# Normalising softmax probabilities on GpSimd before they are turned, in a fused decoder layer

## The chip, the core and the metric

One core of a Trainium2 chip. The time is that of one execution of the whole program in microseconds; lower is better. The kernel before takes 305.01 us, the median of three runs (304.72 to 305.29).

## The reference, cut to what matters

One decoder layer for 256 tokens of width 1024, 16 heads of 64. One projection gives q, k and v. Heads 0 to 7 (group g = 0) attend causally, heads 8 to 15 (g = 1) through a mixture of dilated windows. At this length both are a softmax over a masked row of at most 256 keys:

```
p = softmax(q k^T / 8 + mask)          per head and query
o = p v
o = rmsnorm(o over the group's 512 columns) * gain
x = x + concat(o of both groups) w_out
x = x + (silu(h w_gate) * (h w_up)) w_down,  h = rmsnorm(x) * gain
out = rmsnorm(x) * gain
```

## The kernel before, in words

**Weights.** All products with weights are done in three passes of TensorE: w_hi and w_lo are a rounded weight and its rest, x_hi and x_lo the same of the activation, and hi\*hi, hi\*lo and lo\*hi are added in PSUM (`three_pass`, L431 to L433). Weights come as blocks of 128x512. Blocks 0 to 47 are w_in (six groups of columns of eight blocks; the first four blocks alternate between the first two groups), 48 to 55 w_out for group 0, 56 to 63 for group 1, the rest the feed-forward part. A ring of twelve slots holds them. SP loads four at a time (a quad, `ring_quad`, L356), waiting for lo_ready; ScalarE rounds a pair of blocks (L719), VectorE subtracts (L935, lo_ready), TensorE multiplies (blk_done). ScalarE works nine blocks ahead of its step and VectorE seven.

**Attention.** q and k are rotated on VectorE (`rotate`, L985 to L993: two products into rope_a and rope_b, one sum into rot), turned by TensorE (L458) and split again (L804, L807, L1010, L1013). A tile is 128 queries by 512 columns of scores: tiles 0 and 1 of a group hold four heads each with 128 keys (the first half of the queries), tiles 2 to 5 two heads each with 256 keys. A score item u makes tiles 2u and 2u + 1 in PSUM banks 4 and 5 (L479, L482 to L484). VectorE adds the mask and takes the maximum (L1028, probs, max_ready), ScalarE takes the exponential in place with its sum (L816, sums, exp_done), VectorE turns it in blocks of 32 (L1039, p_squares, p_turned), and SP's four DMAs for each tile bring the blocks to their places (`place_probs`, L397, landed, in_p). Then TensorE multiplies with v (L505, `values`, bank 7), four heads pairs side by side, o turned: columns are queries.

**The sums.** The unnormalised o must be divided by sums that lie one per query and head. VectorE inverts them (L1044), GpSimd widens each to 64 columns (`widen_rsums`, L1230, rope_a and rope_b), TensorE turns them (L519, "rsum", four transposes each), ScalarE copies the result to SBUF (L825, rot), and VectorE multiplies bank 7 by it into o_sb (L1050, "norm"). Then ScalarE makes o_hi (L832) and the squares (L838), VectorE o_lo (L1063), GpSimd adds the squares in two sums (`add_squares`, L1217, L1218), TensorE sums them over partitions ("osum", L526), VectorE and GpSimd make the inverse root (L1055, L1224), which `residual` (L1074) applies to the output projection.

**Order.** Each engine runs its own queue in order. Until block 64, PE_PLAN, DVE_PLAN and ACT_PLAN give, by block number, the items that an engine does at that point; nothing else sets the order. TensorE does the items of a slot behind its block. In the output projection four blocks are done for the first half of the tokens and then for the second, and a slot lies behind each two half blocks. VectorE and ScalarE do the items of slot i and then, for odd i, split the pair that lies seven or nine blocks ahead. PLACE says behind which quad SP puts the four DMAs of which tiles. GpSimd's order is plain code at the end of its part. Semaphores that count tiles or items hold an engine when what it needs isn't there; banks 4 and 5 are written again by a score item only when max_ready says that VectorE has read the last one:

```
done = (g * 3 + u) * 2
if done:
    pe.wait_ge(max_ready, done)
```

Of the kernel before, what the change touches and what calls it, by code (L numbers as in the profile page):

```python
# [24 lines left out]
P = 128  # L25
# [4 lines left out]
GH = GW // HEAD_DIM  # L30
# [37 lines left out]
RSUM_BANK = 7, 6  # L68

NH = NB // 2  # L70
SC_TILES = 6
# [58 lines left out]
    7: [("rope", 0, 0, 0)],  # L130
# [6 lines left out]
    20: [("score", 0, 0), ("turn", 0, 1, 1)],
    24: [("rope", 1, 0, 0), ("squares", 0, 0)],
    25: [("squares", 0, 1), ("score", 0, 1)],
    26: [("rope", 1, 0, 1), ("score", 0, 2)],  # L140
    27: [("squares", 0, 2)],
    28: [("squares", 0, 3)],
    29: [("squares", 0, 4)],
    32: [("rsum", 0, 0), ("turn", 1, 0, 0)],
    33: [("rope", 1, 1, 0), ("squares", 0, 5), ("rope", 1, 1, 1)],
    34: [("turn", 1, 0, 1), ("rsum", 0, 1)],
    37: [("turn", 1, 1, 0)],
    39: [("turn", 1, 1, 1), ("score", 1, 0)],
    40: [("squares", 1, 0), ("squares", 1, 1)],
    41: [("rsum", 1, 0), ("norm", 0, 0), ("score", 1, 1)],  # L150
    42: [("squares", 1, 2)],
    43: [("olo", 0, 0), ("squares", 1, 3), ("norm", 0, 1)],
    45: [("olo", 0, 1), ("score", 1, 2)],
    47: [("squares", 1, 4)],
    48: [("rsum", 1, 1)],
    49: [("squares", 1, 5), ("norm", 1, 0), ("osum", 0)],
    50: [("residual", 0)],
# [9 lines left out]
    11: [("scale", 0), ("scale", 1)],  # L167
    15: [("turn", 0, 0, 0)],
    16: [("turn", 0, 0, 1)],
    21: [("turn", 0, 1, 0)],  # L170
# [4 lines left out]
    31: [("turn", 1, 0, 0)],  # L175
    35: [("turn", 1, 0, 1)],
    36: [("rsum", 0, 0)],
    38: [("turn", 1, 1, 0), ("rsum", 0, 1)],
    39: [("take", 0), ("turn", 1, 1, 1)],
    42: [("score", 1, 0), ("o", 0, 0)],  # L180
    43: [("score", 1, 1)],
    44: [("o", 0, 1)],
    46: [("take", 1), ("score", 1, 2)],
    47: [("rsum", 1, 0)],
    48: [("rsum", 1, 1), ("o", 1, 0)],
    52: [("o", 1, 1)],
    62: [("ffnturn", 0), ("ffnturn", 1), ("residual", 2)],
# [13 lines left out]
def build(nc, x, x_turned, weights, gains, final_norm, table, out):  # L201
# [3 lines left out]
    with ctx:  # L205
# [222 lines left out]
        def _(pe):  # L428
# [16 lines left out]
            def item(it):  # L445
# [40 lines left out]
                elif kind == "values":  # L486
# [5 lines left out]
                    if u == 0:  # L492
                        pe.wait_ge(v_taken, 2 * g + 2)
                        pe.wait_ge(rsum_taken, 2)
                    if u in (0, 1) and g + u:
                        pe.wait_ge(o_ready, g * 2 + half)
                    kb = keys // P

                    for i in range(NB // keys):
                        for b in range(kb):  # L500
                            for r in range(2):
                                T, head = g * SC_TILES + 2 * u + r, attention_tile(2 * u + r)[1][i]
                                x = i * kb + b
                                dst = bank[7][64 * r:64 * r + 64, head // 2 * P:(head // 2 + 1) * P]
# [5 lines left out]
                elif kind == "rsum":  # L510
                    _, g, s = it
                    n = g * 2 + s
                    pe.wait_ge(rsum_wide, n + 1)
                    if n:
                        pe.wait_ge(rsum_taken, n)
                    if n == 2:
                        pe.wait_ge(qk_lo, 8)
                    for p in range(HPAIRS):
                        ins = pe.transpose(bank[RSUM_BANK[g]][:, p * P:(p + 1) * P], rsums_wide[s][:, p * P:(p + 1) * P], ident)  # L519
                    ins.then_inc(rsum_turned, 1)  # L520
# [186 lines left out]
        def _(act):  # L707
# [73 lines left out]
            def item(it):  # L781
# [37 lines left out]
                elif kind == "rsum":  # L819
                    _, g, s = it  # L820
                    act.wait_ge(rsum_turned, g * 2 + s + 1)
                    act.wait_ge(turned, 6)
                    if g:
                        act.wait_ge(o_ready, s + 1)
                    act.activation(rsums_turned[:, s, :], bank[RSUM_BANK[g]][:], ACT.Copy).then_inc(rsum_taken, 1)  # L825
                elif kind == "o":
                    _, g, s = it
                    n = g * 2 + s
                    act.wait_ge(o_ready, n + 1)
                    for k in range(KT // 2):  # L830
                        col = G_MIX + 4 * g + k
                        ins = act.activation(o_hi[:, g * 4 + k, s * P:(s + 1) * P], o_sb[:, g, s, k * P:(k + 1) * P],  # L832
                                             ACT.Copy, scale=gain[:, col:col + 1])
# [4 lines left out]
                    act.activation(o_squares, o_sb[:, g, s, :], ACT.Square).then_inc(o_squared, 1)  # L838
# [90 lines left out]
        def _(dve):  # L929
# [65 lines left out]
            def item(it):  # L995
# [20 lines left out]
                elif kind == "score":  # L1016
# [4 lines left out]
                    for t in (2 * u, 2 * u + 1):  # L1021
# [11 lines left out]
                        ins.then_inc(max_ready, 1)  # L1033
                elif kind == "squares":
                    T = it[1] * SC_TILES + it[2]
                    dve.wait_ge(exp_done, T + 1)
# [4 lines left out]
                elif kind == "rsum":  # L1041
                    _, g, half = it
                    dve.wait_ge(exp_done, g * SC_TILES + (SC_TILES if half else 2))
                    dve.reciprocal(rsums[:, g, half, :], sums[:, g, half, :]).then_inc(rsum_ready, 1)  # L1044
                elif kind == "norm":
                    _, g, half = it
                    n = g * 2 + half
                    dve.wait_ge(rsum_taken, n + 1)
                    dve.wait_ge(valued, g * 3 + (3 if half else 1))
                    dve.tensor_tensor(o_sb[:, g, half, :], bank[7][:], rsums_turned[:, half, :],  # L1050
                                      ALU.mult).then_inc(o_ready, 1)
# [5 lines left out]
                elif kind == "olo":  # L1057
                    _, g, s = it
                    dve.wait_ge(ot_hi, g * 2 + s + 1)
                    for k in range(KT // 2):  # L1060
                        col = G_MIX + 4 * g + k
                        at = (slice(None), g * 4 + k, slice(s * P, (s + 1) * P))
                        ins = dve.scalar_tensor_tensor(o_lo[at], o_sb[:, g, s, k * P:(k + 1) * P], gain[:, col:col + 1],  # L1063
# [260 lines left out]
```

## Time and profile before

| what | us |
|---|---|
| median of three runs | 305.01 (304.72 to 305.29) |
| the profiled execution | 304.64 |
| its span | 302.8 |
| TensorE busy | 294.3 |
| VectorE busy | 202.8 |
| ScalarE busy | 167.2 |
| GpSimd busy | 18.8 |

The span is what the profiler saw between the first and the last instruction; the execution's own time has 1.84 us more around it. PE is the matmul side of TensorE, PEld its weight loads, DVE is VectorE, ACT ScalarE, POOL GpSimd, SP the queue that issues most DMAs. Busy times of matmuls overlap, since they are pipelined, so the start of the next one tells more than the length of one. A line such as L935 is a line of the kernel. "slot" and "step" below are the keys of the plans.

### The profile page before, as it was taken

What the parts mean: (1) busy time and instruction counts of PE and PEld (TensorE: products, weight loads), DVE (VectorE), ACT (ScalarE), POOL (GpSimd) and SP (SyncE); (2) the same over time, 40 slices, a digit from 0 to 9 for tenths busy, and PEclk for the clock granted to TensorE, in tenths of its full rate; (3) what the DMA queues carried; (4) which work ended last, traced back from release to release, by engine and by line L of the source; (5) the groups of instructions that cost most, each with busy time, mean ns of one, the idle gap of its engine ahead of it and who ended that gap; (6) DMA issues with size and microseconds to landing.
All of it is one profiled execution on the core that took longest, in us unless ns stands there. A gap on an engine that the chain in (4) does not pass through costs nothing.

```text
span 302.8 us, 4343 instructions
## 1 busy us (share of the span) xinstructions
PE 294.3 (97%) x1449; PEld 239.6 (79%) x1449; DVE 202.8 (67%) x332; ACT 167.2 (55%) x283; POOL 18.8 (6%) x29
## 2 busy tenths in 40 slices
PE   6999999999999999999999999999999999999992
PEld 2788877887778788888888888888888888888882
DVE  3879999987886789729755555637465655455454
ACT  4877775739686557817554445354362545444224
POOL 0002000030313220200000000000000000000010
PEclk9999999999999999999999999999999999999998
DMA  6999563852577635765866567565656575651003
GB/s 181 384 427 355 192 219 106 273 123 123 159 246 235 266 141 154 273 234 207 263 274 208 226 182 268 173 240 175 213 172 242 179 267 161 233 204 28 0 0 139
DMA packets 22620, 61.65 MB, mean 204 GB/s; under 512 B 2640, under 2 KB 14160, under 8 KB 16720
## 3 DMA queue, kind: packets, MB, share of 16 engines
q1 hardware_dynamic: 22176, 60.70, 57.5%
q10 hardware_dynamic: 432, 0.80, 0.7%
q8 instruction: 7, 0.11, 0.2%
q14 instruction: 5, 0.04, 0.0%
HBM read 54.67 MB, written 1.05 MB: 184 GB/s over the span
## 4 chain that ended last, share of the span: by engine, by line
PE 94%; DMA 2%; issue 1%; DVE 1%; ACT 1%; SPq 0%; POOL 0%; POOLq 0%; DVEq 0%; ACTq 0%
PE bank L431 30%; PE bank L433 29%; PE bank L432 29%; PE bank L505 2%; DMA raw<-in_weights 2%; PE bank L458 1%; PE bank L479 1%; PE bank L519 1%; PE bank L482 1%; PE bank L441 1%; DVE xs L1148 0%; PE bank L483 0%; PE bank L484 0%; ACT rot L923 0%; DVE w_lo L963 0%
## 5 line engine op out<-in xcount | busy, mean ns | idle before, releaser
L719 ACT ACTIVATE w_hi<-raw 128x1024 fp32r<-128x1024 f32 x94 | 97.7, 1056 | 80.8 <-PE bank L433 72.7
L935 DVE TENSOR_TENSOR w_lo<-raw,w_hi 128x1024 fp32r<-128x1024 f32 x94 | 112.0, 1214 | 17.9 <-ACT w_hi L719 16.6
L431 PE MATMUL bank<-w_hi,x_hi 128*128 128x512 f32 x270 | 107.0, 396 | 0.2 <-DVE w_lo L963 0.2
L433 PE MATMUL bank<-w_hi,x_lo 128*128 128x512 f32 x270 | 105.3, 390 | 0.0
L432 PE MATMUL bank<-w_lo,x_hi 128*128 128x512 f32 x270 | 105.2, 390 | 0.0
L431 PEld LDWEIGHTS bank<-w_hi,x_hi 128*128 128x128 f32 x270 | 50.7, 188 | 11.9 <-DVE w_lo L963 0.9
L433 PEld LDWEIGHTS bank<-w_hi,x_lo 128*128 128x128 f32 x270 | 50.7, 188 | 10.9
L432 PEld LDWEIGHTS bank<-w_lo,x_hi 128*128 128x128 f32 x270 | 50.7, 188 | 9.9
L431 PE MATMUL bank<-w_hi,h_hi 128*128 128x512 f32 (+1 forms) x82 | 31.6, 385 | 0.0
L433 PE MATMUL bank<-w_hi,h_lo 128*128 128x512 f32 (+1 forms) x82 | 31.5, 384 | 0.0
L432 PE MATMUL bank<-w_lo,h_hi 128*128 128x512 f32 (+1 forms) x82 | 31.5, 384 | 0.0
L1091 DVE SCALAR_TENSOR_TENSOR rope_a<-bank,rstd,rope_b 128x256 f32<-128x256 f32 x22 | 9.8, 480 | 30.4 <-ACT rope_b L858 30.3
L1109 DVE TENSOR_TENSOR h_lo<-landed,h_hi 128x512 fp32r<-128x512 f32 x10 | 6.9, 692 | 23.6 <-ACT h_hi L863 23.6
L433 PEld LDWEIGHTS bank<-w_hi,h_lo 128*128 128x128 f32 x82 | 15.4, 188 | 3.1
L432 PEld LDWEIGHTS bank<-w_lo,h_hi 128*128 128x128 f32 x82 | 15.4, 188 | 3.0
L431 PEld LDWEIGHTS bank<-w_hi,h_hi 128*128 128x128 f32 x82 | 15.4, 188 | 3.0
L816 ACT ACTIVATE probs<-probs,neg_max 128x128 f32<-128x128 f32 (+1 forms) x32 | 14.1, 447 | 4.8 <-DVE neg_max L1028 4.8
L431 PE MATMUL bank<-w_hi,o_hi 128*128 128x512 f32 (+1 forms) x42 | 16.5, 393 | 0.0
L432 PE MATMUL bank<-w_lo,o_hi 128*128 128x512 f32 (+1 forms) x42 | 16.0, 380 | 0.0
L433 PE MATMUL bank<-w_hi,o_lo 128*128 128x512 f32 (+1 forms) x42 | 16.0, 380 | 0.0
L858 ACT ACTIVATE rope_b<-bank,rstd 128x256 f32<-128x256 f32 x22 | 9.6, 465 | 4.1 <-PE bank L433 4.1
L1206 POOL TENSOR_SCALAR msq<-ssq 128x2 f32<-128x2 f32 (+1 forms) x2 | 0.4, 192 | 174.4 <-ACT junk L750 174.4
(101 smaller groups left out, 244.0 us busy)
## 6 DMA issues: line engine op xcount, KB each, us to landing
raw<-in_weights SPq DMA_DIRECT2D x46, 1024.0 KB, 4.8
landed<-p_squares SPq DMA_DIRECT2D x88, 64.0 KB, 2.1
raw<-in_weights SPq DMA_DIRECT2D x4, 512.0 KB, 8.0
raw<-in_weights SPq DMA_DIRECT2D x4, 256.0 KB, 4.9
xs<-in_x SPq DMA_DIRECT2D x2, 512.0 KB, 10.5
o_sb<-in_x_turned SPq DMA_DIRECT2D x3, 256.0 KB, 7.0
out<-rot SPq DMA_DIRECT2D x3, 256.0 KB, 2.0
vals<-in_final_norm ACTq DMA_DIRECT2D x1, 512.0 KB, 6.0
```

The source lines that it names most:

```text
L431: pe.matmul(dst, a_hi, w1, start=first, stop=False)
L432: pe.matmul(dst, a_hi, w2, start=False, stop=False)
L433: return pe.matmul(dst, a_lo, w1, start=False, stop=last)
L441: ins = pe.transpose(dst[:, a * SEQ + s * P:a * SEQ + (s + 1) * P], xs[:, s, kt * P:(kt + 1) * P], ident)
L458: ins = pe.transpose(bank[TURN_BANK[qk_i][s]][:, p * P:(p + 1) * P], rot[:, qk_i, s, p * P:(p + 1) * P], ident_ja if qk_i else ident)
L505: ins = pe.matmul(dst.rearrange("p (i b) -> p i b", b=SQ), vals[:, g, b, head * HEAD_DIM:(head + 1) * HEAD_DIM], landed[:, T % LANDINGS, : ...
L719: act.activation(w_hi[:, slot:slot + 2, :], raw[:, slot:slot + 2, :], ACT.Copy).then_inc(hi_ready, 1)
L816: ins = act.activation(piece, piece, ACT.Exp, bias=neg_max[:, g, half, head:head + 1], scale=-1.0, accum_out=sums[:, g, half, head:head + 1])
L858: act.activation(silu[:, s, :], bank[4 + s][:, 0:FC], ACT.Silu, scale=rstd[:, 6 + s:7 + s]).then_inc(silu_done, 1)
L935: dve.tensor_tensor(w_lo[:, slot:slot + 2, :], raw[:, slot:slot + 2, :], w_hi[:, slot:slot + 2, :].bitcast(f32), ALU.subtract).then_inc(lo ...
L1091: dve.scalar_tensor_tensor(hid[:, s, :], bank[4 + s][:, FC:2 * FC], rstd[:, 6 + s:7 + s], silu[:, s, :], ALU.mult, ALU.mult).then_inc(hid_ ...
L1109: dve.tensor_tensor(hidden[1], placed, hidden[0].bitcast(f32), ALU.subtract).then_inc(ht_lo, 1)
```

## The change

The probabilities are normalised before they are turned. VectorE inverts the sums of each pair of tiles ("invert"), GpSimd multiplies each tile of probs in place by them, one instruction for each head (`normalise`, p_normed), and the turning in blocks waits for that instead of for the exponential. Then bank 7 (first half of the queries) and bank 6 (second half) hold the finished o: ScalarE takes o_hi and VectorE o_lo straight from the bank, and ScalarE's squares become an item of their own ("osq") that waits for o_lo. The widening, the turning of the sums, their copy and the product are gone. A values item waits for the squares that were read from its bank. The three plans and PLACE are made anew.

```diff
-RSUM_BANK = 7, 6
+VALUE_BANK = 7, 6
 PE_PLAN = {
-    16: [("turn", 0, 0, 0)],
-    17: [("turn", 0, 0, 1)],
-    20: [("turn", 0, 1, 0), ("turn", 0, 1, 1)],
+    17: [("turn", 0, 0, 0)],
+    18: [("turn", 0, 0, 1)],
+    19: [("turn", 0, 1, 0), ("turn", 0, 1, 1)],
     21: [("score", 0, 0)],
     24: [("score", 0, 1)],
-    28: [("score", 0, 2)],
-    32: [("turn", 1, 0, 0)],
-    35: [("turn", 1, 0, 1)],
-    38: [("turn", 1, 1, 0), ("rsum", 0, 0), ("turn", 1, 1, 1)],
-    39: [("rsum", 0, 1)],
-    40: [("score", 1, 0)],
-    41: [("values", 0, 0), ("score", 1, 1)],
-    43: [("values", 0, 1)],
-    45: [("values", 0, 2), ("rsum", 1, 0)],
-    46: [("score", 1, 2)],
+    29: [("score", 0, 2)],
+    30: [("turn", 1, 0, 0)],
+    36: [("turn", 1, 0, 1)],
+    38: [("turn", 1, 1, 0), ("turn", 1, 1, 1)],
+    40: [("score", 1, 0), ("score", 1, 1)],
+    41: [("values", 0, 0)],
+    45: [("values", 0, 1), ("values", 0, 2), ("score", 1, 2)],
     49: [("values", 1, 0)],
-    51: [("rsum", 1, 1), ("osum", 0), ("values", 1, 1)],
-    54: [("values", 1, 2)],
+    51: [("osum", 0), ("values", 1, 1)],
+    55: [("values", 1, 2)],
     58: [("osum", 1)],
     61: [("ffnturn", 0), ("ffnturn", 1)],
 }
 DVE_PLAN = {
-    7: [("rope", 0, 0, 0)],
+    5: [("rope", 0, 0, 0)],
...
+    20: [("turn", 0, 1, 1), ("score", 0, 0)],
+    22: [("invert", 0, 0), ("rope", 1, 0, 0)],
+    23: [("score", 0, 1)],
+    24: [("squares", 0, 0)],
+    25: [("rope", 1, 0, 1), ("squares", 0, 1)],
+    27: [("invert", 0, 1), ("score", 0, 2), ("squares", 0, 2)],
+    29: [("invert", 0, 2)],
+    30: [("squares", 0, 3)],
+    31: [("squares", 0, 4)],
+    32: [("turn", 1, 0, 0)],
+    33: [("squares", 0, 5), ("rope", 1, 1, 0), ("rope", 1, 1, 1)],
+    35: [("turn", 1, 0, 1)],
     37: [("turn", 1, 1, 0)],
     39: [("turn", 1, 1, 1), ("score", 1, 0)],
+    40: [("invert", 1, 0), ("squares", 1, 0), ("score", 1, 1), ("squares", 1, 1)],
+    42: [("invert", 1, 1), ("squares", 1, 2)],
+    43: [("olo", 0, 0)],
     45: [("olo", 0, 1), ("score", 1, 2)],
+    46: [("squares", 1, 3)],
+    47: [("invert", 1, 2)],
+    48: [("squares", 1, 4), ("osum", 0)],
+    49: [("squares", 1, 5), ("olo", 1, 0)],
     50: [("residual", 0)],
+    52: [("residual", 1)],
+    54: [("olo", 1, 1)],
+    56: [("osum", 1)],
+    57: [("residual", 2)],
...
 ACT_PLAN = {
...
+    40: [("score", 1, 0)],
+    41: [("score", 1, 1), ("o", 0, 0)],
+    43: [("o", 0, 1), ("osq", 0, 0)],
+    44: [("osq", 0, 1)],
+    45: [("take", 1), ("score", 1, 2)],
+    47: [("o", 1, 0)],
+    51: [("osq", 1, 0)],
     52: [("o", 1, 1)],
+    55: [("osq", 1, 1)],
+    60: [("residual", 2)],
+    62: [("ffnturn", 0), ("ffnturn", 1)],
 }
-PLACE = {(3, 0): (0,), (3, 1): (1,), (3, 2): (2, 3, 4, 5), (4, 0): (6,), (4, 1): (7, 8), (5, 0): (9, 10, 11)}
+PLACE = {(3, 0): (0, 1), (3, 1): (2,), (3, 2): (3, 4, 5), (4, 0): (6,), (4, 1): (7, 8), (4, 2): (9,), (5, 0): (10, 11)}
@@ TensorE, values
-                        pe.wait_ge(rsum_taken, 2)
-                    if u in (0, 1) and g + u:
-                        pe.wait_ge(o_ready, g * 2 + half)
+                    if g and u in (0, 1):
+                        pe.wait_ge(o_squared, half + 1)
+                    elif u == 1:
+                        pe.wait_ge(qk_lo, 8)
-                                dst = bank[7][64 * r:64 * r + 64, ...]
+                                dst = bank[VALUE_BANK[half]][64 * r:64 * r + 64, ...]
@@ ScalarE
                 elif kind == "o":
                     _, g, s = it
-                    act.wait_ge(o_ready, n + 1)
+                    act.wait_ge(valued, g * 3 + (3 if s else 1))
...
+                elif kind == "osq":
+                    _, g, s = it
+                    n = g * 2 + s
+                    act.wait_ge(ot_lo, n + 1)
                     if n:
                         act.wait_ge(o_added, n)
                     act.wait_ge(turned, 8)
+                    act.activation(o_squares, bank[VALUE_BANK[s]][:], ACT.Square).then_inc(o_squared, 1)
@@ VectorE
+                elif kind == "invert":
+                    _, g, u = it
+                    half, heads, _ = attention_tile(2 * u)
+                    some = slice(heads[0], heads[0] + 2 * len(heads))
+                    dve.wait_ge(exp_done, g * SC_TILES + 2 * u + 2)
+                    dve.reciprocal(rsums[:, g, half, some], sums[:, g, half, some]).then_inc(inverted, 1)
                 elif kind == "squares":
-                    dve.wait_ge(exp_done, T + 1)
+                    dve.wait_ge(p_normed, T + 1)
@@ GpSimd
-            widen_rsums(0)
-            widen_rsums(1)
-            widen_rsums(2)
+            def normalise(T):
+                g, t = T // SC_TILES, T % SC_TILES
+                half, heads, keys = attention_tile(t)
+                pool.wait_ge(inverted, T // 2 + 1)
+                for i, head in enumerate(heads):
+                    piece = probs[:, T % 4, i * keys:(i + 1) * keys]
+                    ins = pool.tensor_scalar(piece, piece, rsums[:, g, half, head:head + 1], None, ALU.mult)
+                ins.then_inc(p_normed, 1)
+
+            for T in range(SC_TILES + 4):
+                normalise(T)
             add_squares(0)
             add_squares(1)
-            widen_rsums(3)
+            for T in range(SC_TILES + 4, 2 * SC_TILES):
+                normalise(T)
             inverse_rms_of_o(0)
             add_squares(2)
             add_squares(3)
```

## Rows read from the trace of the kernel before

**Rows 1.** The page: busy times, and the chain by engine.

```profile
PE 294.3 (97%) x1449; PEld 239.6 (79%) x1449; DVE 202.8 (67%) x332; ACT 167.2 (55%) x283; POOL 18.8 (6%) x29
PE 94%; DMA 2%; issue 1%; DVE 1%; ACT 1%; SPq 0%; POOL 0%; POOLq 0%; DVEq 0%; ACTq 0%
```

**Rows 2.** PE's two longest waits: total us, times, longest.

```profile
PE bank L541 <- ACT w_hi L725: 1.3, 1, 1.3
PE bank L591 <- DVE warm L930: 1.2, 1, 1.2
```

**Rows 3.** The chain in order of time, two of L519's four pieces: start us, us.

```profile
69.10 0.44 PE bank L519 x4
...
83.69 0.59 PE bank L519 x4
```

**Rows 4.** PE's timeline behind slot 24: start us, us, what.

```profile
44.88 0.50 PE L431 MATMUL bank<-w_hi,x_hi 128*128 128x512 f32 x1
45.22 0.40 PE L432 MATMUL bank<-w_lo,x_hi 128*128 128x512 f32 x1
```

**Rows 5.** Timelines around the first rotation, of VectorE and of PE.

```profile
21.20 0.68 DVE L985 TENSOR_TENSOR rope_a<-bank,tab 128x512 f32<-128x512 f32 x1
...
23.13 1.22 DVE L935 TENSOR_TENSOR w_lo<-raw,w_hi 128x1024 fp32r<-128x1024 f32 x1
...
20.32 0.39 PE L431 MATMUL bank<-w_hi,x_hi 128*128 128x512 f32 x1
...
23.04 0.39 PE L431 MATMUL bank<-w_hi,x_hi 128*128 128x512 f32 x1
```

**Rows 6.** VectorE's timeline, four pieces of 256 keys, first row and what follows.

```profile
52.03 0.42 DVE L1028 CUSTOM_DVE_ANT_0 probs<-bank,tab 128x256 f32<-128x256 f32 x1
...
53.41 0.71 DVE L1039 STREAM_TRANSPOSE p_squares<-probs 128x512 f32<-128x512 f32 x1
```

**Rows 7.** The same for eight pieces of 128 keys.

```profile
72.78 0.28 DVE L1028 CUSTOM_DVE_ANT_0 probs<-bank,tab 128x128 f32<-128x128 f32 x1
...
74.46 1.22 DVE L935 TENSOR_TENSOR w_lo<-raw,w_hi 128x1024 fp32r<-128x1024 f32 x1
```

**Rows 8.** Timelines of PE, VectorE, ScalarE, GpSimd from values(1,2) to osum(1).

```profile
100.95 1.09 PE L505 MATMUL bank<-landed,vals 128*64 128x128 f32 x16
101.98 0.50 PE L431 MATMUL bank<-w_hi,o_hi 128*128 128x512 f32 x1
...
107.55 0.50 PE L526 MATMUL bank<-ones,rot 128*128 128x1 f32 x4
...
102.16 0.69 DVE L1050 TENSOR_TENSOR o_sb<-bank,rot 128x512 f32<-128x512 f32 x1 [0.89 <-PE bank L505]
...
102.89 1.28 ACT L832 ACTIVATE o_hi<-o_sb,gain 128x128 fp32r<-128x128 f32 x4 [3.34 <-DVE o_sb L1050]
104.07 0.61 ACT L838 ACTIVATE rot<-o_sb 128x512 f32<-128x512 f32 x1
...
105.76 1.53 POOL L1218 TENSOR_TENSOR rot<-rot 128x128 f32<-128x128 f32 x1
```

**Rows 9.** GpSimd: two copies by time; the sums by line, ns min/median/max.

```profile
64.32 1.47 POOL L1230 COPY rope_a<-rsums 128x512 f32<-128x512 f32 x1 [39.13 <-DVE rot L993]
...
77.97 0.61 POOL L1230 COPY rope_a<-rsums 128x512 f32<-128x512 f32 x1 [10.38 <-DVE rsums L1044]
...
L1217 POOL TENSOR_TENSOR rot<-rot x4: 744/916/1197, 80.4 to 104.8; 128x256 f32<-128x256 f32 x4
...
L1218 POOL TENSOR_TENSOR rot<-rot x4: 461/466/1535, 81.7 to 105.8; 128x128 f32<-128x128 f32 x4
```

**Rows 10.** Issue to landing, 40 to 110 us: quads' median, then the tiles' DMAs.

```profile
raw<-in_weights SPq DMA_DIRECT2D x10, 1024.0 KB, 5.2
...
DMA to landing us min/median/max: 2.0/2.5/7.0
```

**Rows 11.** Window behind PE's waits: PE, PEld, DVE, ACT, POOL busy, PEclk, DMA.

```profile
8.00:10.00 2.00, 2.00 (x10) 1.59 (x10) 1.52 (x4) 1.45 (x3) 0.00 (x0) 1.00 0.99 367
```

More of the change, by code:

```diff
@@ L133 @@
     15: [("rope", 0, 1, 1)],
-    16: [("turn", 0, 0, 0)],
-    17: [("turn", 0, 0, 1)],
+    17: [("turn", 0, 0, 0), ("turn", 0, 0, 1)],
     19: [("turn", 0, 1, 0)],
[L137 to L145, printed above, removed]
@@ L164 @@
+    56: [("osum", 1)],
+    57: [("residual", 2)],
+    60: [("ffnturn", 0)],
+    61: [("ffnturn", 1), ("residual", 3)],
 }
 ACT_PLAN = {
[L167 to L170, printed above, removed]
+    13: [("scale", 0)],
+    14: [("scale", 1)],
+    17: [("turn", 0, 0, 0)],
+    18: [("turn", 0, 0, 1)],
+    20: [("turn", 0, 1, 0)],
     23: [("turn", 0, 1, 1)],
@@ L174 @@
     28: [("score", 0, 2)],
-    31: [("turn", 1, 0, 0)],
+    29: [("turn", 1, 0, 0)],
     35: [("turn", 1, 0, 1)],
-    36: [("rsum", 0, 0)],
-    38: [("turn", 1, 1, 0), ("rsum", 0, 1)],
+    38: [("turn", 1, 1, 0)],
     39: [("take", 0), ("turn", 1, 1, 1)],
[L180 to L185, printed above, removed]
+    40: [("score", 1, 0)],
[5 more added lines that the diff above has]
+    51: [("osq", 1, 0)],
     52: [("o", 1, 1)],
-    62: [("ffnturn", 0), ("ffnturn", 1), ("residual", 2)],
+    55: [("osq", 1, 1)],
+    60: [("residual", 2)],
+    62: [("ffnturn", 0), ("ffnturn", 1)],
 }
-PLACE = {(3, 0): (0,), (3, 1): (1,), (3, 2): (2, 3, 4, 5), (4, 0): (6,), (4, 1): (7, 8), (5, 0): (9, 10, 11)}
+PLACE = {(3, 0): (0, 1), (3, 1): (2,), (3, 2): (3, 4, 5), (4, 0): (6,), (4, 1): (7, 8), (4, 2): (9,), (5, 0): (10, 11)}
 def attention_tile(u_tile):
@@ L503, in item @@
                                 x = i * kb + b
-                                dst = bank[7][64 * r:64 * r + 64, head // 2 * P:(head // 2 + 1) * P]
+                                dst = bank[VALUE_BANK[half]][64 * r:64 * r + 64, head // 2 * P:(head // 2 + 1) * P]
                                 ins = pe.matmul(dst.rearrange("p (i b) -> p i b", b=SQ),
@@ L509, in item @@
                     ins.then_inc(valued, 1)
[L510 to L520, printed above, removed]
                 elif kind == "osum":
@@ L818, in item @@
                         ins.then_inc(exp_done, 1)
[L819 to L825, printed above, removed]
                 elif kind == "o":
                     _, g, s = it
[L828 to L829 removed]
+                    act.wait_ge(valued, g * 3 + (3 if s else 1))
                     for k in range(KT // 2):
                         col = G_MIX + 4 * g + k
[L832 removed]
+                        ins = act.activation(o_hi[:, g * 4 + k, s * P:(s + 1) * P],
+                                             bank[VALUE_BANK[s]][:, k * P:(k + 1) * P],
                                              ACT.Copy, scale=gain[:, col:col + 1])
                     ins.then_inc(ot_hi, 1)
+                elif kind == "osq":
+                    _, g, s = it
+                    n = g * 2 + s
+                    act.wait_ge(ot_lo, n + 1)
                     if n:
@@ L1062, in item @@
                         at = (slice(None), g * 4 + k, slice(s * P, (s + 1) * P))
-                        ins = dve.scalar_tensor_tensor(o_lo[at], o_sb[:, g, s, k * P:(k + 1) * P], gain[:, col:col + 1],
-                                                       o_hi[at].bitcast(f32), ALU.mult, ALU.subtract)
+                        ins = dve.scalar_tensor_tensor(o_lo[at], bank[VALUE_BANK[s]][:, k * P:(k + 1) * P],
+                                                       gain[:, col:col + 1], o_hi[at].bitcast(f32), ALU.mult, ALU.subtract)
                     ins.then_inc(ot_lo, 1)
```

41 lines of the change are left out of this document (2 added, 39 removed).

## The prediction

> **What bounds the kernel now.** I read the page's busy shares and chain first, then who waits for whom, then each engine's timeline around every slot that the change touches. TensorE is busy for 294.3 of 302.8 us and carries 94% of the chain that ended last [rows 1]. Its two waits of more than 0.2 us, 1.3 and 1.2, lie at the start, on the first weights [rows 2]. So from 8 us to 291 us whatever is taken off TensorE is won at its full length, whatever makes it wait is lost at its full length, and work moved between the other engines counts only through such a wait. I therefore price TensorE's removed work first and then walk the new tables slot by slot: at a slot, when does TensorE arrive, and when is what it waits for there?
>
> The profiled execution took 304.64 us (span 302.8 and 1.84 around it); the three runs have a median of 305.01. I work in differences and add them to the median.
>
> **Removed from TensorE.** The sixteen transposes of the sums stand in the chain as four pieces, three of 0.44 and one of 0.59: 3 x 0.44 + 0.59 = 1.91 us [rows 3]. All of it is on the path: **-1.9 us**. Where TensorE changes from split blocks to an item and back, a pitch is longer: 44.88 to 45.22, 0.34 instead of 0.23 [rows 4]. The new table has two such changes fewer (43 and 46 go into 45), some 0.2 to 0.4 us, of which I count nothing. Four L1050 products on VectorE (0.69) and four L825 copies on ScalarE, about as long, go too [rows 8]; none is on the path, so they are worth nothing by themselves, except where a slot below names them.
>
> **Slot 5, the first rotation moved from 7.** ("rope", 0, 0, 0) waits for blk_done 10, that is for block 9 (QKV_DONE[0] = 10). The first matmul after block 9 starts at 20.32, so the wait ends near 20.5. Before, VectorE did the split of blocks 12 and 13 ahead of it, and the rotation came at 21.20. Now the rotation comes first, and the split queues behind it: 20.5 + 1.93 (21.20 to 23.13, the rotation's pitch) = 22.4, + 1.22 for the split = 23.65. TensorE wants blocks 12 and 13 at 23.04 [rows 5]. It was never late there; now it waits about 0.65. **+0.65 us** (0.4 to 0.8).
>
> **Slot 30.** The turn of group 1's q needs max_ready 6, so all of VectorE's ("score", 0, 2). Before, four blocks lay between that score (28) and the turn (32); now one, 1.4 us. VectorE starts about 0.12 us after the last score matmul (the pause that L1050 shows at 102.16 behind L505 [rows 8]) and its four pieces take 52.03 to 53.41 = 1.38 and 0.08 for the last accumulator, 1.58 in all [rows 6]. 1.58 - 1.4 = **+0.15 us**. VectorE must be free when the score lands: counting its queue from the exponentials of tile 1 it is, with a few tenths to spare; if not, up to 0.6.
>
> **Slot 40.** Here ("score", 1, 0) and ("score", 1, 1) stand side by side. Both write banks 4 and 5, so the second waits for max_ready 8: VectorE's eight pieces of the first. Before, block 41 and the first values, 2.5 us, lay between. Now nothing does. The wait is 0.12 + (74.46 - 72.78 = 1.68) + 0.08 + a wake of 0.05 to 0.1 [rows 7] = **+1.95 us** (1.8 to 2.2). No later slot can fill it, since TensorE's queue is in order. It also leaves the values behind it waiting for nothing.
>
> **Slots 55 and 58, the end of o.** Let V be the start of the matmul behind values(1,2): 101.98 before. TensorE comes to osum(1) 24 matmuls later (107.55, so 0.232 each); now values(1,2) stands two half blocks later while osum(1) stays, so 18 matmuls or 4.18 us are left. The chain that must fit, before: L1050 102.16, o_hi 102.89 to 104.17, squares 104.07 to 104.68 beside o_lo, two GpSimd sums to 107.29 [rows 8]; 5.3 us against 5.6. Now L1050 is gone (-0.7) but the squares wait for o_lo, as both engines read the same bank. VectorE has residual(1) (blk_done 56, about V - 1.05, 1.33 long) and a split (1.14) ahead of o_lo, which so starts near V + 1.4, when o_hi (V + 0.1, + 1.28) is just done. o_lo from PSUM has one SBUF operand less, 4 x 0.27 = 1.1: V + 2.55. That meets TensorE's second halves of block 56 (12 matmuls, V + 2.8) without a wait. Squares to V + 3.2. The next split, V + 2.5 to 3.7, keeps GpSimd from its first sum, which took 1.20 in such a place and 0.74 at best [rows 9]: done V + 4.3; the second 0.46 + 0.08 and a wake: V + 4.9. 4.9 - 4.2 = **+0.75 us** (0.3 to 1.7, the upper end if a split meets the second sum as at 105.76, 1.53 instead of 0.46). Before, squares and o_lo overlapped, in SBUF. The Trainium skill ("PSUM — Partial Sum Buffer", "PSUM bank collisions raise a hardware error") says that two engines reading one bank at the same time collide; no run here shows it. With that rule the wait has to stay; were it dropped the 0.75 would vanish and the sum would be 0.85 us instead of 1.6.
>
> **Added on GpSimd.** Twelve tiles of 512 columns. No row has this operation. Below: the one-input copy of 512 columns, 0.61. Above: the two-input sums, 0.46 for 128 columns, so 4 x 0.54 = 2.2 with gaps [rows 9]. One input tensor makes the copy nearest, but each piece has a start of its own; I take 1.5 for a tile of four pieces, about the middle, and 1.0 for one of two. Against VectorE's operations with two SBUF inputs it waits: 0.61 became 1.47 at 64.32, beside a split [rows 9]. What covers it: by VectorE's queue tiles 2 to 5 are ready when their transposes come up, or up to 0.5 late, and the split of blocks 40 and 41 behind them ends near 66.7 against 69 where TensorE wants it. The six reciprocals have the same cover. SP's queue: place 0 and 1 now stand ahead of the quad of blocks 40 to 43 (issued near 54.5, landed 5.2 later [rows 10], needed at 69); place 9 ahead of that of 60 to 63 (issued near 93, needed near 109). The tightest are tiles 10 and 11, behind ("osum", 0) on VectorE: from block 47's end, tile 11 is turned at 8.0, SP's four issues follow tile 10's and end at 11.3, the last lands 2.0 to 2.5 after its issue at 10.7 [rows 10], so 12.7 to 13.2; TensorE wants it at 13.9. Cost nothing, with 0.7 us to spare.
>
> **Sum.** -1.9 + 0.65 + 0.15 + 1.95 + 0.75 = **+1.6 us**: 306.6. Steps added at their ends: -1.9 + 0.4 + 0 + 1.8 + 0.3 = +0.6 and -1.9 + 0.8 + 0.6 + 2.2 + 1.7 = +3.4.
>
> **The rivals.** (B) **GpSimd late.** If a tile takes 2.2 us and splits push it further, tiles 10 and 11 come over 1 us later; behind the 0.7 of cover values(1,2) waits, place holds SP, and block 40's split may slip as well: 1.4 us on top, +3.0 or 308.0. It decides once a tile passes about 1.8 us. For it: the contended rows, 1.47 and 1.53 for work of 0.61 and 0.46. Against: only some two tiles meet a split. The Trainium skill ("GPSIMD Engine Reference", "Key points") says that GpSimd shares its SBUF interfaces with VectorE's instructions of two SBUF inputs, and that VectorE is about twice as fast on elementwise work. The trace agrees on the first.
> (C) **Not slower.** TensorE's changes between kinds of matmul cost more than their long pitches, and the two merged slots give back what the waits take. If each change costs a quarter of a microsecond in all, two of them are 0.5. With the waits at their low ends it is 0.6 - 0.5 = +0.1, or 305.1. It decides where the small waits (slots 5, 30 and 58) are together under about 0.9 instead of 1.55. For it: the wake times are my reading, and GpSimd's second sum was held once in four times [rows 9]. Against: slot 5 and slot 40 are bare sums of rows.
> (D) **Faster.** The transposes' time is won and the bank wait does not show in full, for instance because a record of the scores misleads on when banks are read: -1.9 + 0.65 = -1.25, 303.75. Against it: the semaphore wait stands in the code and the eight pieces' time in the rows.
>
> **How the numbers follow.** Forecast 0.55, B 0.18, C 0.18, D 0.09. Less than 0.2% (0.61 us) can't be told from no change. The forecast and B are slower: 0.73; C is the same: 0.18; D faster: 0.09. The range takes in the forecast, C down to -0.3 us and B up to its own value: 304.7 to 308.0, leaving out D and half of B, 0.17.
>
> **What would show it.** TensorE's waits: L431 on VectorE's w_lo near 23 us (0.65); the turn L458 near 55 (0.15); L482 on L1028's neg_max near 73 (1.95), the longest of the kernel; L526 on GpSimd near 108 (0.75); L519 gone. A GpSimd tile of four pieces 1.5 us. Wrong would be: no wait of L482; a wait at L505 (that is B); or a TensorE pitch other than 0.23 after the stalls, which the granted clock of 1.00 behind the 1.3 us wait at the start [rows 2, 11] speaks against.

## The result, and the profile after

The changed kernel takes **309.56 us** (median of four runs, 309.01 to 310.56) against 305.03: a ratio of 1.0147 with an interval of 1.0132 to 1.0161. It is slower, as forecast, but by 4.5 us where I had 1.6; 309.56 lies above the range of 304.7 to 308.0. A second measurement gave 309.39 (1.0134, 1.0119 to 1.0149). The profiled execution took 309.61 us, its span is 307.8.

The page of the changed kernel, busy times and chain by engine, against [rows 1]:

```profile
PE 293.9 (96%) x1433; PEld 238.4 (77%) x1433; DVE 200.3 (65%) x330; ACT 165.4 (54%) x279; POOL 42.7 (14%) x57
...
PE 78%; DVE 9%; POOL 4%; issue 3%; DMA 2%; ACT 2%; SPq 1%; POOLq 0%; DVEq 0%; ACTq 0%
```

TensorE's share of the chain fell from 94% to 78%; VectorE and GpSimd are now part of it. So the chain runs through waits. All that TensorE waited for in the changed kernel (us in total, times, longest), against [rows 2]:

```profile
PE bank L477 <- DVE neg_max L1010: 2.5, 1, 2.5
PE bank L501 <- issue: 1.4, 1, 1.4
PE bank L576 <- DVE warm L912: 1.2, 1, 1.2
PE bank L453 <- DVE rot L975: 0.9, 1, 0.9
PE bank L511 <- POOL rot L1195: 0.6, 1, 0.6
PE bank L426 <- DVE w_lo L917: 0.5, 1, 0.5
PE bank L426 <- DVE w_lo L945: 0.5, 1, 0.5
PE bank L526 <- ACT w_hi L710: 0.4, 1, 0.4
```

The start (L576, L945, L526) belongs to no edit: the first matmul of block 10 began anywhere between 20.32 and 21.77 us in the traces of this case, and in two of them whose tables are those of the kernel before up to there, at 20.32 and at 21.43. Here it began at 20.90, 0.58 later than in the trace of the kernel before. The other five waits are 0.53 + 0.88 + 2.49 + 1.35 + 0.61 = 5.86 us; with the 0.58 and less 1.9 for the transposes that is 4.5 of the 5.0 us by which the span grew. The idle time in brackets is a little short of the price: it begins at a matmul's recorded end, 0.39 us after its start, where the next one else starts after 0.23, so a wait behind one of them costs up to 0.16 more. Their places in TensorE's timeline (start, us, in brackets the idle time before):

```profile
24.30 0.50 PE L426 MATMUL bank<-w_hi,x_hi 128*128 128x512 f32 x1 [0.53 <-DVE w_lo L917]
...
69.33 0.66 PE L453 MATMUL bank<-tab,rot 128*128 128x128 f32 x4 [0.88 <-DVE rot L975]
76.32 0.39 PE L477 MATMUL bank<-qkT_hi 64*128 64x256 f32 x2 [2.49 <-DVE neg_max L1010]
99.71 1.09 PE L501 MATMUL bank<-landed,vals 128*64 128x128 f32 x16 [1.35 <-issue]
112.43 0.61 PE L511 MATMUL bank<-ones,rot 128*128 128x1 f32 x4 [0.61 <-POOL rot L1195]
```

Counting each trace from the start of block 10 to the end of its span leaves the start out. By that count the kernel before takes 282.5 us (302.8 - 20.32), the changed one 286.9 (307.8 - 20.90), and the second trace of the changed kernel (below) 286.9 as well: 4.4 us more. I give this count below as "from block 10"; it is one trace for each kernel.

| place | forecast | measured |
|---|---|---|
| slot 5, split behind the rotation | 0.65 | 0.53 |
| slot 30, turn behind score | 0.15 | 0 |
| slot 38, turn of k | 0 | 0.88 |
| slot 40, banks 4 and 5 | 1.95 | 2.49 |
| slot 51, values(1,1) | 0 | 1.35 |
| slot 58, osum(1) | 0.75 | 0.61 |

The small steps were right within 0.15 us. The extra is at slots 38, 40 and 51, and what stands in front of them is GpSimd. For slot 51 the profile names no releaser ("issue"); I read the wait as that for tile 9, whose four DMAs SP issued only until 98.10, 1.6 us before the values began; the profile's page has 2.1 us from the issue of such a DMA to its landing:

```profile
94.66 3.44 SPq L392 DMA_DIRECT2D landed<-p_squares  x4
```

GpSimd's timeline in the changed kernel, the multiplications alone, against [rows 9]:

```profile
45.83 5.93 POOL L1209 TENSOR_SCALAR probs<-probs,rsums 128x128 f32<-128x128 f32 x8 [19.89 <-DVE rsums L1021]
54.56 9.95 POOL L1209 TENSOR_SCALAR probs<-probs,rsums 128x256 f32<-128x256 f32 x8 [2.80 <-DVE rsums L1021]
78.88 4.66 POOL L1209 TENSOR_SCALAR probs<-probs,rsums 128x128 f32<-128x128 f32 x8 [14.37 <-DVE rsums L1021]
85.58 3.62 POOL L1209 TENSOR_SCALAR probs<-probs,rsums 128x256 f32<-128x256 f32 x4 [2.04 <-DVE rsums L1021]
```

Eight pieces of 128 keys are two tiles of four heads; four pieces of 256 are two tiles of two heads, eight are four. Where little stands against it, a tile costs 2.3 us (4.66 / 2) or 1.8 (3.62 / 2); beside VectorE's splits, 3.0 (5.93 / 2) or 2.5 (9.95 / 4). I had 1.5 and 1.0. VectorE's queue shows what that does, since its turning in blocks now waits for GpSimd:

```profile
61.38 0.71 DVE L1027 STREAM_TRANSPOSE p_squares<-probs 128x512 f32<-128x512 f32 x1 [1.10 <-POOL probs L1209]
...
64.54 0.71 DVE L1027 STREAM_TRANSPOSE p_squares<-probs 128x512 f32<-128x512 f32 x1 [0.74 <-POOL probs L1209]
...
68.58 0.69 DVE L975 TENSOR_TENSOR rot<-rope_a,rope_b 128x512 f32<-128x512 f32 x1
69.19 1.22 DVE L917 TENSOR_TENSOR w_lo<-raw,w_hi 128x1024 fp32r<-128x1024 f32 x1
```

Tiles 4 and 5 stand ahead of group 1's rotations of k in that queue, so the last rotation ended at 69.27 and TensorE's turn of it began at 69.33. The theory (G) after this reading: GpSimd's duration makes the extra. The rival (T): the new tables do, whatever GpSimd takes.

### The profile page after: what moved, and what is told of

Read it like the earlier page. It is cut to its first block, busy times and chain, and to the rows that moved or that the text cites. A ratio compares the mean times of both kernels' runs of the same rounds, so it can differ in the third digit from the quotient of the medians.

```text
span 307.8 us, 4318 instructions
## 1 busy us (share of the span) xinstructions
PE 293.9 (96%) x1433; PEld 238.4 (77%) x1433; DVE 200.3 (65%) x330; ACT 165.4 (54%) x279; POOL 42.7 (14%) x57
## 4 chain that ended last, share of the span: by engine, by line
PE 78%; DVE 9%; POOL 4%; issue 3%; DMA 2%; ACT 2%; SPq 1%; POOLq 0%; DVEq 0%; ACTq 0%
PE bank L426 25%; PE bank L428 25%; PE bank L427 24%; POOL probs L1209 3%; DVE w_lo L917 2%; DMA raw<-in_weights 2%; PE bank L501 2%; DVE probs L1010 1%; DVE rope_b L969 1%; ACT probs L801 1%; DVE rot L975 1%; DVE rope_a L967 1%; PE bank L436 1%; PE bank L453 1%; DVE xs L1051 0%
## 5 line engine op out<-in xcount | busy, mean ns | idle before, releaser
L426 PE MATMUL bank<-w_hi,x_hi 128*128 128x512 f32 x270 | 106.8, 395 | 1.0 <-DVE w_lo L917 0.5
L426 PEld LDWEIGHTS bank<-w_hi,x_hi 128*128 128x128 f32 x270 | 50.7, 188 | 13.1 <-DVE w_lo L945 1.3
L1209 POOL TENSOR_SCALAR probs<-probs,rsums 128x128 f32<-128x128 f32 (+1 forms) x32 | 28.7, 914 | 40.3 <-DVE rsums L1021 40.3
L426 PE MATMUL bank<-w_hi,h_hi 128*128 128x512 f32 (+1 forms) x82 | 31.6, 385 | 0.0
L426 PEld LDWEIGHTS bank<-w_hi,h_hi 128*128 128x128 f32 x82 | 15.4, 188 | 3.0
L426 PE MATMUL bank<-w_hi,o_hi 128*128 128x512 f32 (+1 forms) x42 | 16.5, 392 | 0.0
```

The costliest lines, as they stand in the source:

```text
L426: pe.matmul(dst, a_hi, w1, start=first, stop=False)
L1209: ins = pool.tensor_scalar(piece, piece, rsums[:, g, half, head:head + 1], None, ALU.mult)
```

## The experiments

**GpSimd nearly free.**

```diff
-                for i, head in enumerate(heads):
-                    piece = probs[:, T % 4, i * keys:(i + 1) * keys]
+                for i, head in list(enumerate(heads))[:1]:
+                    piece = probs[:, T % 4, i * keys:i * keys + 2]
```

Expected: 

> The changed kernel, but GpSimd multiplies only the first two columns of each tile, so it leaves out nearly all of the normalising and keeps every wait and table. Theory G (GpSimd's multiplication, 0.6 us for 128 columns and 0.9 for 256 and more beside splits, is what came on top of the forecast): TensorE's wait for the turn at slot 38 (0.88) and the one for landed at values(1,1) (1.35) go, the one for banks 4 and 5 falls from 2.49 to about 1.95, the other waits stay; 309.6 - 2.8 = 306.8 us. Rival T (the tables and the new order of placing alone make those waits): all stay within 0.3, 309.0 to 309.6.

Measured: 306.75 us (1.0063, 1.0038 to 1.0087). TensorE's waits behind the start:

```profile
PE bank L477 <- DVE neg_max L1010: 2.0, 1, 2.0
...
PE bank L511 <- POOL rot L1195: 0.6, 1, 0.6
...
PE bank L426 <- DVE w_lo L917: 0.5, 1, 0.5
```

Slots 38 and 51 are clean, slot 40 stands at 1.97, and these are the waits of my forecast, with its time (306.6). Theory G holds: 2.8 us of the 4.5 come from how long GpSimd takes. From block 10 it is 283.8 us, 1.3 more than the kernel before and 3.1 less than the changed one.

**The price of the operation.** Each piece copied onto itself instead of multiplied:

```diff
-                    ins = pool.tensor_scalar(piece, piece, rsums[:, g, half, head:head + 1], None, ALU.mult)
+                    ins = pool.tensor_copy(piece, piece)
```

Expected: 

> The changed kernel, but each of GpSimd's 32 pieces is copied onto itself instead of multiplied (no normalising; left out). It prices the operation: if copying goes at the rate of the widening before (0.61 us for 512 columns), a piece takes 0.25 to 0.4 us and the kernel 306.8 to 307.2, so the price was the multiplication by a scalar from SBUF. Rival: reading and writing one buffer or small pieces is what costs; pieces stay at 0.6 and 0.9 us and the time at 309.5.

Measured: 307.3 us (306.1 to 308.07 over five runs; 1.0073, 1.005 to 1.0096). The pieces by line, in ns (min/median/max), first of the changed kernel and then of this one:

```profile
L1209 POOL TENSOR_SCALAR probs<-probs,rsums x32: 597/918/2279, 45.8 to 99.1; 128x128 f32<-128x128 f32 x16, 128x256 f32<-128x256 f32 x16
```

```profile
L1209 POOL COPY probs<-probs x32: 292/396/1393, 45.3 to 93.8; 128x128 f32<-128x128 f32 x16, 128x256 f32<-128x256 f32 x16
```

A single piece takes half as long when it is copied: 292 ns against 597 at the least. Piece behind piece the gain is larger, since the records of copies overlap. Two tiles of four heads, with little against them:

```profile
76.81 1.96 POOL L1209 COPY probs<-probs 128x128 f32<-128x128 f32 x8 [17.25 <-DVE rsums L1021]
```

That is 0.98 us for a tile that takes 2.3 (4.66 / 2) when it is multiplied. Same buffers, same sizes, so the price lies in multiplying by a scalar from SBUF; whether in the multiplication or in its scalar operand, no run separates. It grows by 2.5 ns with each further column (3.62 / 4 = 0.905 for 256 columns, less 4.66 / 8 = 0.583 for 128). That is near the slope of the two-input sums (0.744 - 0.461 for 128 columns, 2.2 ns [rows 9]).

**VectorE's queue order alone.** GpSimd untouched, tiles 4 and 5 turned behind the rotations:

```diff
-    31: [("squares", 0, 4)],
-    33: [("squares", 0, 5), ("rope", 1, 1, 0), ("rope", 1, 1, 1)],
-    35: [("turn", 1, 0, 1)],
+    33: [("rope", 1, 1, 0), ("rope", 1, 1, 1)],
+    35: [("turn", 1, 0, 1), ("squares", 0, 4)],
+    36: [("squares", 0, 5)],
-PLACE = {..., (3, 2): (3, 4, 5), (4, 0): (6,), ...}
+PLACE = {..., (3, 2): (3,), (4, 0): (4, 5, 6), ...}
```

Expected: 

> The changed kernel with VectorE's turning of tiles 4 and 5 moved from steps 31 and 33 (ahead of the rotations) to 35 and 36 (behind them), and their placing behind the next quad. GpSimd is untouched. If the 0.88 us wait at slot 38 comes from VectorE's queue being held for GpSimd's tiles 4 and 5 in front of the rotations, it goes, and the bank wait falls from 2.49 to about 2.0 since VectorE reaches score (1, 0) in time: 308.1 us, or 307.5 where no clock is lost behind a shorter wait. Rival: GpSimd's tiles are late for whatever stands behind them, and the hold moves on to the turn of k or to the splits: no gain, 309 or more.

Measured: 307.46 us (306.74 to 308.67; 1.0074, 1.0045 to 1.0103). The wait at slot 38 is gone, the one for the banks 1.97:

```profile
74.15 0.54 PE L477 MATMUL bank<-qkT_hi 64*128 64x256 f32 x2 [1.97 <-DVE neg_max L1010]
```

The granted clock behind it fell here, and tile 9's wait is missing:

```profile
74.00:76.00 2.00, 1.85 (x13) 1.66 (x14) 1.14 (x2) 2.00 (x12) 0.00 (x0) 0.56 0.04 11
```

So here the slow GpSimd tiles cost by what was queued behind the instruction that waited for them: moving the turning of two tiles, with their placing, gave back 2.1 us of the 2.8 by the medians. From block 10 it is 285.4 us, 1.5 under the changed kernel, about the 0.88 and the 0.5 that went.

**The two scores apart.**

```diff
-    40: [("score", 1, 0), ("score", 1, 1)],
-    41: [("values", 0, 0)],
+    40: [("score", 1, 0)],
+    41: [("values", 0, 0), ("score", 1, 1)],
```

Expected: 

> The changed kernel with one item moved back: TensorE's score (1, 1) behind values (0, 0) at slot 41 instead of directly behind score (1, 0) at slot 40. If the bank wait of 2.49 us is what it looks like, 2.5 us of other work hide it and nothing takes its place: wait under 0.3, time 307.2 to 307.6. Rival: the time comes back as a later wait, since VectorE needs these scores for tile 9 in time: values(1,1) waits up to 2 us longer and the time stays within 0.6 of 309.6.

Measured: 310.64 us (309.46 to 312.21; 1.0187, 1.0144 to 1.023), so there is no gain, as the rival had it, though its 0.6 us around 309.6 was too narrow. The 2.49 us wait is gone. What TensorE waits for instead is the three rows of L501 and 0.5 us at block 48 (L426, issue); the 0.9 of slot 38 was there before:

```profile
PE bank L501 <- ACT vals L774: 1.3, 1, 1.3
...
PE bank L501 <- DMA landed<-p_squares: 1.0, 1, 1.0
PE bank L453 <- DVE rot L975: 0.9, 1, 0.9
PE bank L501 <- issue: 0.8, 1, 0.8
...
PE bank L426 <- issue: 0.5, 1, 0.5
```

values(1,0) waits for v, (1,1) and (1,2) for their tiles. From block 10 it is 286.8 us against 286.9: the move changed nothing, and the longer time of this trace lies ahead of block 10, which began at 21.77 and not at 20.90. I read this as follows: with GpSimd as slow as it is, the chain from group 1's scores to its values sets the time, and the bank wait stood beside that chain, not on top of it. The same move with the two-column GpSimd tests it:

Expected: 

> The two-column run (normalising left out but for two columns of a tile) and score (1, 1) back at slot 41, both. The scores apart alone made no gain (310.6 against 309.6), with waits at the values instead. Theory G: those waits are there because GpSimd makes the chain from scores to values as long as the tables allow; with GpSimd short the 1.97 us bank wait is a pure loss and goes: 304.8 us. Rival T: the chain is too long even so (turning, placing, taking v), the wait comes back at the values: 306.3 or more.

Measured: 304.35 us (0.9979, 0.9969 to 0.9989), 2.4 less than with the scores together, and no wait but the start, slot 5 and slot 58 (from block 10 281.8 against 283.8 us, 2.0 less):

```profile
PE bank L511 <- POOL rot L1195: 0.6, 1, 0.6
PE bank L426 <- DVE w_lo L917: 0.5, 1, 0.5
```

So the wait at slot 40 is worth 2.0 to 2.4 us where GpSimd is short and nothing where it isn't. The two causes are not a sum.

**Slots 5 and 58 alone.**

```diff
-    5: [("rope", 0, 0, 0)],
+    7: [("rope", 0, 0, 0)],
```

Expected: 

> The changed kernel with VectorE's first rotation back at step 7. The 0.53 us wait of L426 for w_lo at 24.3 goes: 309.0 to 309.2 us. Rival: the rotation later makes the turns later and the wait moves to the first turn; no gain.

```diff
-    58: [("osum", 1)],
+    59: [("osum", 1)],
```

Expected: 

> The changed kernel with TensorE's osum (1) one slot later (59 instead of 58). The 0.61 us wait for GpSimd's sums goes, since 1.4 us of block 59 come before it: 309.0. Rival: the inverse root and the residual come later by that and TensorE waits for the first turn of the feed-forward part instead: no gain or up to 0.3 slower.

Measured: 308.49 (1.0105, 1.0087 to 1.0122) and 308.38 us (1.0102, 1.0085 to 1.0119). Each took its wait out of the trace (0.53 and 0.61) and put nothing in its place. The medians fell by half a microsecond more than that, but from block 10 both are at 286.1 us against 286.9, 0.8 less: the idle time and the up to 0.16 that it is short. In both traces the granted clock fell behind the 2.48 us wait at slot 40 (0.50 and 0.63 from 76 to 78 us), and tile 9's wait is missing.

**The bank wait in the kernel before.** The two-line edit of slots 40 and 41, the other way round and in the kernel before.

Expected: 

> The kernel before with one item moved: score (1, 1) directly behind score (1, 0) at slot 40, as in the changed kernel. It measures that slot alone, without GpSimd's part. Bank theory: a wait of 1.9 to 2.1 us for max_ready at that score, nothing else changes, 307.0 us. Rival: other engines' earlier data give part of it back and the time is under 306.3.

Measured: 310.46 us (308.93 to 311.12; 1.0161, 1.0125 to 1.0196), 5.5 slower for a wait of 2.66. Neither expectation holds. The stretches around the wait, in this kernel's trace (busy time of each engine, then the granted clock, DMA share, GB/s):

```profile
70.00:73.00 3.00, 3.00 (x27) 2.35 (x25) 1.83 (x2) 2.97 (x6) 0.00 (x0) 1.00 0.54 224
73.00:75.80 2.80, 0.14 (x5) 0.03 (x1) 2.52 (x18) 2.80 (x8) 0.00 (x0) 0.92 0.00 0
75.80:78.00 2.20, 2.20 (x14) 1.88 (x15) 1.61 (x2) 2.20 (x14) 0.00 (x0) 0.50 0.00 0
78.00:80.00 2.00, 2.00 (x6) 1.30 (x4) 0.80 (x2) 0.19 (x2) 0.62 (x1) 0.50 0.00 0
80.00:82.00 2.00, 2.00 (x17) 1.58 (x16) 0.00 (x0) 0.00 (x0) 0.00 (x0) 0.50 0.00 0
82.00:84.00 2.00, 2.00 (x11) 1.56 (x9) 1.67 (x8) 0.94 (x4) 0.00 (x0) 0.96 0.12 32
```

The wait is longer than the 1.95 of the arithmetic because score(1,0) ended near 73.1 and VectorE came to it only at 73.89, behind its share of the turn of k (L1013 at 73.28, released by ScalarE's copy of it, which stood behind the two of v).

TensorE stood still for 2.66 us, and the granted clock is then 0.50, 1.2 GHz of 2.4, until 82 us, 6 us long. The matmuls show it (78.83 to 79.25, 0.43 apart, not 0.23; then again 0.23):

```profile
78.83 0.63 PE L431 MATMUL bank<-w_hi,x_hi 128*128 128x512 f32 x1
79.25 0.63 PE L432 MATMUL bank<-w_lo,x_hi 128*128 128x512 f32 x1
...
83.18 0.39 PE L432 MATMUL bank<-w_lo,x_hi 128*128 128x512 f32 x1
83.41 0.39 PE L433 MATMUL bank<-w_hi,x_lo 128*128 128x512 f32 x1
```

Six us at half the clock do the work of three: about 3 us lost behind a wait of 2.66, together about the 5.5 (from block 10 287.8 against 282.5 us, 5.3 more).

**Is the clock part of the changed kernel's time?** Its first trace has 1.00 in every stretch from 4 to 287 us. The same kernel once more:

Expected: 

> The changed kernel once more, untouched, for a second trace of it. In its first trace the granted clock was 1.00 throughout and TensorE waited 1.35 us for landed at values(1,1); in the traces of three variants with the same 2.5 us bank wait the clock stood near 0.5 for 2 to 4 us behind it and that wait was missing. Clock theory: the two are alternatives, each 1 to 2 us, so that a trace has one or the other and the time is 309.5 either way. Rival: the clock's fall is a loss of its own on top: a trace with both, and over 310.5 us.

Measured: 309.39 us (309.21 to 310.16). The second trace, behind the same 2.47 us wait:

```profile
78.00:80.00 2.00, 2.00 (x6) 1.28 (x4) 0.20 (x1) 1.06 (x6) 0.61 (x2) 0.52 0.00 0
80.00:82.00 2.00, 2.00 (x18) 1.56 (x18) 0.23 (x1) 0.00 (x0) 2.00 (x4) 0.63 0.00 0
82.00:84.00 2.00, 2.00 (x9) 1.66 (x10) 1.84 (x9) 0.81 (x3) 2.00 (x4) 1.00 0.08 20
```

The clock fell (a loss of 2 x 0.48 + 2 x 0.37 = 1.7 us), and values(1,1) has no wait. The first trace had no fall and 1.35 us of that wait. From block 10 both take 286.9 us. That is what the clock theory said: TensorE comes to tile 9 late by the clock, or early and waits for it. Over the eight runs of both measurements, the three with a mean clock of 0.999 took 309.01, 309.21 and 309.61, the five with 0.990 to 0.992 309.36 to 310.56, 0.5 more on average. So the two are alternatives for the most part; whether wholly the medians leave open. Three more traces have the same wait at slot 40, 2.47 to 2.48 us (first rotation at 7, osum(1) at 59, and the next experiment). In all three the clock fell and tile 9's wait is missing, so it fell in four traces of five.

**VectorE normalises instead.** One broadcast product of a tile in front of its turning; GpSimd's `normalise` is no longer called (`whole` is the tile of probs, split by heads):

```diff
+                    dve.tensor_tensor(whole, whole, rsums[:, it[1], half, heads[0]:heads[-1] + 1:2]
+                                      .unsqueeze(2).to_broadcast([P, len(heads), keys]), ALU.mult).then_inc(p_normed, 1)
                     dve.wait_ge(p_normed, T + 1)
```

Expected: 

> The changed kernel with its tables, but VectorE does the normalising itself: one product of a tile (512 columns) with its inverse sums, spread, right in front of the turning; GpSimd's multiplications are gone. Theory G: what cost time was GpSimd's duration (1.8 to 2.9 us for a tile), so 0.65 us a tile on VectorE brings nearly what the two-column run brought: 306.8 to 307.5, no wait at slot 38 over 0.3. Rival D: VectorE is the scarce engine here, 7.5 us more on it make splits or rotations late and the wait at slot 38 stays or grows: 308.5 or more.

Measured: 311.69 us (1.0217, 1.019 to 1.0243). Rival D was right: the product takes 0.68 us, about as thought, but VectorE has no room for it in group 0. It comes late to the scores that slot 30 waits for, and slot 38 waits as before:

```profile
57.90 0.63 PE L453 MATMUL bank<-tab,rot 128*128 128x128 f32 x4 [1.47 <-DVE neg_max L1010]
...
71.20 0.66 PE L453 MATMUL bank<-tab,rot 128*128 128x128 f32 x4 [0.86 <-DVE rot L975]
```

Slot 30 is the one that broke (1.47, 0 in the changed kernel). In group 1 there was no wait at slot 51, which suggested to share the work. It doesn't show that VectorE has room there: the clock fell in this trace too (0.50 from 78.2 to 80 us), and behind such a fall tile 9's wait was missing in the other traces of these tables too.

**Versions put together.** Group 0 on GpSimd, group 1 on VectorE (the product above under `if it[1]:`), the scores apart, tiles 4 and 5 behind the rotations, the first rotation at 7, osum(1) at 59:

Expected: 

> A version put together from what the runs showed: GpSimd normalises group 0 only, VectorE group 1 (a broadcast product of 0.68 us a tile, in place of 6.5 us in which it waited for GpSimd), tiles 4 and 5 turned behind the rotations, score (1, 1) at slot 41, the first rotation at 7, osum (1) at 59. If the transposes' 1.9 us can be had once no item of the table is late: waits only at the start, 303.1 us (the two-column run with scores apart, 304.35, less 0.5 and 0.6). Rival: GpSimd's group 0 or VectorE's longer queue in group 1 makes one of splits, turns or values late: 304.5 or more.

Measured: **304.05 us** (0.9962, 0.994 to 0.9985), between the 303.1 that I expected and the rival's 304.5, with one wait left behind the start, for tile 9:

```profile
95.24 1.09 PE L501 MATMUL bank<-landed,vals 128*64 128x128 f32 x16 [1.52 <-issue]
```

And with tile 9 turned at step 43:

```diff
-    43: [("olo", 0, 0)],
+    43: [("olo", 0, 0), ("squares", 1, 3)],
-    46: [("squares", 1, 3)],
```

Expected: 

> The shared version (304.05 us) with one more move: VectorE turns tile 9 at step 43 instead of 46, so it is placed 3 us earlier. The 1.5 us wait of values(1,1) at 95.2, the only one left behind the start, goes; TensorE then waits for nothing between 10 and 290 us: 302.6 us. Rival: the transposed tile only pushes the split and o_lo of steps 43 and 45 back and TensorE waits at slot 48 for o_lo or the weights: 304 or more.

Measured: **303.8 us** (303.68 to 304.29; 0.9957, 0.9944 to 0.9969), 1.4 us under the 305.16 of the kernel before beside it. It is faster than both kernels, but 1.2 above what I expected: the 1.52 went and other waits came:

```profile
PE bank L500 <- DMA landed<-p_squares: 0.9, 1, 0.9
...
PE bank L500 <- ACT vals L773: 0.2, 1, 0.2
```

values(1,2) waits 0.90 for the last tile, values(1,0) 0.25 for v. Of TensorE's work nothing but the transposes is gone against the kernel before, and 1.4 us are won of their 1.9 (from block 10 281.4 against 282.5 us, 1.1). Five edits went into the first of these versions at once. None ran with these tables and GpSimd on both groups, so what the sharing alone brings is open.

## Why the prediction was wrong

**Removed from TensorE, -1.9.** Held, as a saving: in the last version 1.4 of it was kept, and 1.15 us of waits stand against it there.

**Slots 5, 30 and 58.** Right: 0.53, 0 and 0.61 for 0.65, 0.15 and 0.75. The edits that undo 5 and 58 take their waits away.

**Slot 40.** The mechanism was right and the wait without GpSimd's part is 1.97 (forecast 1.95). The 2.49 of the changed kernel has 0.5 that is GpSimd's: VectorE came late to score(1,0). As a price the 1.95 was right only where GpSimd is short (2.0 to 2.4). In the changed kernel moving the score back brought nothing (310.64), because the wait stood beside a chain through GpSimd that was too long anyway.

**Added on GpSimd, "Cost nothing".** This is the step that failed. I took 1.5 and 1.0 us for a tile, about midway between the copy and the two-input sums, and called the whole cost nothing; the tile costs 2.3 and 1.8 with little against it and 3.0 and 2.5 on average beside splits. The upper bound of 2.2 from the two-input sums was the right neighbour. It was just short of the 2.3, and well short beside splits, because VectorE's splits can hold each piece anew: the five pieces over 1.3 us (1.37 to 2.28) all ran beside one. They lie in five tiles, where I had counted on "only some two". For comparison, VectorE's product of a whole tile takes 0.68 us where GpSimd takes 1.8 to 2.3, 2.6 to 3.4 times as long: the Trainium skill ("GPSIMD Engine Reference", "Key points"), which calls VectorE about twice as fast on elementwise work, has the direction that the trace shows and is low in size here. And I looked at the wrong queue: I gave tiles 4 and 5 "up to 0.5" of lateness and called the split behind them covered, but it was the rotations behind them, needed at slot 38. Behind both, the values of tile 9, which I had at nothing, waited too. In all 0.88 + 0.5 + 1.35 = 2.7 us, nearly the 2.8 between 309.56 and 306.75.

**Rival B** had the mechanism (a tile over 1.8 us decides, a wait at the values' matmuls), at a chance of 0.18 and 308.0. Its price was 1.4 instead of 2.8; it named tiles 10 and 11, and tile 9 was late. The range stopped at B's 308.0, though the steps at their upper ends came to +3.4, which is 308.4; and D with half of B is 0.18, not 0.17. Neither changes that 309.56 lies outside.

**The clock.** I took the 1.00 behind the 1.3 us wait at the start as speaking against a fall behind 1.95. That was no evidence for a longer wait: the clock fell behind 2.47 to 2.49 us in four traces of five, and behind 1.97 us in the kernel with its queue reordered (0.56 in the stretch behind it), but not behind 1.97 in the trace of the two-column kernel or 2.02 in that of the copying one. In the changed kernel's total it mostly takes the place of tile 9's wait; in the kernel before with the two scores together it doubled the loss.

## What to carry to other kernels

Price an operation on GpSimd from a row of the same kind of operation, a scalar operand from SBUF included, and then ask which instruction of another engine waits for it and what is queued behind that one: here moving the turning of two tiles gave back half or more of what GpSimd's slowness had cost. A wait in a matmul queue that is dense otherwise can cost twice its length, as 2.66 us did in the kernel before, since the clock may fall behind it. A wait found in a trace is a price only if the work behind it would be ready earlier: take it away in one run before it is added up. And where the start differs from one execution to the next, count from a matmul behind it: single traces then told apart what the medians blurred.

## What the runs showed of the hardware that I had not expected

- GpSimd's multiplication by a scalar from SBUF: 597 ns for 128 columns at the least, 583 from one piece to the next; 905 from one to the next for 256. Copying the same pieces: 292 at the least, 245 (1.96 / 8) from one to the next for 128 columns.
- The granted clock fell to 0.50 behind a TensorE wait of 2.66 us and stayed there for 6 us; behind 2.47 to 2.49 it fell in four traces of five, the same kernel once and once not; behind 1.97 to 2.02 in one of three.
- ScalarE's o_hi from PSUM took 1.10 to 1.14 us for four pieces where it took 1.26 to 1.28 from SBUF, and VectorE's o_lo 1.08 to 1.12 where two of its four before had taken 1.63 beside GpSimd.
